# Gate and up products with token rows as output, in the FFNs of a three-block fp32 transformer kernel

## The reference

```
def rmsnorm(x, g):
    xf = x.astype(jnp.float32)
    y = xf * lax.rsqrt(jnp.mean(xf * xf, axis=-1, keepdims=True) + EPS)
    return (y * g.astype(jnp.float32)).astype(x.dtype)

def swiglu(h, w_gate, w_up, w_down):
    return (jax.nn.silu(h @ w_gate) * (h @ w_up)) @ w_down

x = x + 0.5 * swiglu(rmsnorm(x, ffn1_norm[i]), ffn1_w_gate[i], ffn1_w_up[i], ffn1_w_down[i])
```

## Time and profile before

| what | value |
|---|---|
| median of 3 runs | 2114.19 us (2111.84 to 2114.88) |
| span of the profiled execution | 2110.5 us |
| own time of the profiled execution | not reported beside its span |
| PE busy | 1841.2 us, 87% of the span |
| PE weight loads busy | 1364.1 us, 65% |
| DVE busy | 802.8 us, 38% |
| ACT busy | 598.7 us, 28% |
| POOL busy | 133.3 us, 6% |
| granted TensorE clock, mean of the span | 0.924 |
| DMA | 603.95 MB, mean 286 GB/s |

### The profile page before, as it was taken

The page is one execution under the profiler, slowest core; times in us unless marked ns, Lnnn a source line. Parts: engine busy times, 40 slices in busy tenths (PEclk is TensorE's granted clock), DMA queues, the critical chain, the costliest instruction groups (busy, mean ns, idle before and its releaser), DMA issues.

```text
span 2110.5 us, 30801 instructions
## 1 busy us (share of the span) xinstructions
PE 1841.2 (87%) x13330; PEld 1364.1 (65%) x13330; DVE 802.8 (38%) x940; ACT 598.7 (28%) x705; POOL 133.3 (6%) x140
## 2 busy tenths in 40 slices
PE   8999999999999999999999986676777677777766
PEld 8999997999999997699999831222223212122221
DVE  6556556655756564766568500000000000000000
ACT  5334546443433355643347300000000000000001
POOL 4100011400000000220002000000000000000000
PEclk9999999999999999999999987898787879788788
DMA  7555552455555554065566999999999999999998
GB/s 260 189 181 170 162 185 98 168 179 179 201 165 194 195 168 145 21 209 180 179 205 210 423 409 427 429 427 428 429 429 428 428 429 429 428 428 428 429 428 347
DMA packets 182536, 603.95 MB, mean 286 GB/s; under 512 B 11952, under 2 KB 139440, under 8 KB 158016
## 3 DMA queue, kind: packets, MB, share of 16 engines
q1 hardware_dynamic: 180560, 601.43, 73.5%
q10 hardware_dynamic: 1648, 0.96, 0.2%
q0 software_dynamic: 256, 0.52, 0.1%
HBM read 601.84 MB, written 1.05 MB: 286 GB/s over the span
## 4 chain that ended last, share of the span: by engine, by line
PE 59%; DMA 36%; DVE 2%; ACT 1%; issue 1%; SPq 0%; ACTq 0%; POOL 0%; DVEq 0%; POOLq 0%
PE ps L1045 21%; DMA bulk<-in_w_up 17%; PE ps L1059 12%; DMA bulk<-in_w_down 8%; DMA bulk<-in_w_gate 8%; PE ps L1222 3%; PE ps L1618 3%; DMA keep<-in_w_up 2%; PE ps L1644 2%; DMA keep<-in_w_down 2%; PE ps L1116 2%; PE ps L1011 2%; PE ps L1115 2%; PE ps L1117 2%; PE ps L1239 1%; PE ps L1577 1%
## 5 line engine op out<-in xcount | busy, mean ns | idle before, releaser
L1045 PE MATMUL ps<-part,part 128*128 128x256 f32 x3840 | 460.2, 280 | 0.4 <-DVE part L2212 0.4
L1045 PEld LDWEIGHTS ps<-part,part 128*128 128x128 f32 x3840 | 455.5, 188 | 1.0 <-DVE part L2212 0.8
L1618 PE MATMUL ps<-bulk 128*32 128x512 f32 x1616 | 255.8, 765 | 150.6 <-DMA bulk<-in_w_up 93.0
L2212 DVE TENSOR_TENSOR part<-bulk,part 128x2048 fp32r<-128x2048 f32 x88 | 202.9, 2347 | 255.5 <-ACT part L1710 255.5
L1618 PEld LDWEIGHTS ps<-bulk 128*32 128x32 f32 x1616 | 50.8, 125 | 339.4 <-issue 135.1
L1059 PE MATMUL ps<-part,part 128*128 128x256 f32 x2112 | 255.5, 280 | 0.0
L1059 PEld LDWEIGHTS ps<-part,part 128*128 128x128 f32 x2112 | 251.8, 188 | 0.2 <-issue 0.2
L1710 ACT ACTIVATE part<-bulk 128x2048 fp32r<-128x2048 f32 x86 | 160.1, 1910 | 258.0 <-DMA bulk<-in_ffn_w_up 243.8
L2785 DVE TENSOR_TENSOR keep<-keep,ps 128x512 f32<-128x512 f32 x16 | 11.0, 687 | 544.0 <-PE ps L1618 544.0
L1644 PE MATMUL ps<-bulk,keep 128*32 128x512 f32 x784 | 109.4, 693 | 23.6 <-DMA bulk<-in_w_down 23.0
L2221 DVE TENSOR_TENSOR part<-bulk,part 128x2048 fp32r<-128x2048 f32 x46 | 105.6, 2311 | 46.0 <-ACT part L1725 46.0
(11 more groups left out here) (309 smaller groups left out, 2229.8 us busy)
## 6 DMA issues: line engine op xcount, KB each, us to landing
bulk<-in_w_gate SPq DMA_DIRECT2D x53, 2048.0 KB, 40.7
bulk<-in_w_up SPq DMA_DIRECT2D x48, 2048.0 KB, 39.7
bulk<-in_w_down SPq DMA_DIRECT2D x48, 2048.0 KB, 40.2
bulk<-in_ffn_w_gate SPq DMA_DIRECT2D x44, 1024.0 KB, 7.5
bulk<-in_ffn_w_up SPq DMA_DIRECT2D x44, 1024.0 KB, 10.0
bulk<-in_ffn_w_down SPq DMA_DIRECT2D x44, 1024.0 KB, 5.2
keep<-in_w_up SPq DMA_DIRECT2D x16, 2048.0 KB, 40.7
keep<-in_w_down SPq DMA_DIRECT2D x15, 2048.0 KB, 40.4
```

The source lines that it names most:

```text
L1045: ins = pe.matmul(y, w_, x_, start=(k == m == 0), stop=(k == KD - 1 and m == 2))
L1618: ins = pe.matmul(ps[j * CAP:(j + 1) * CAP, half, :], xe[:, k, :], w[:, kk, j * HALF:(j + 1) * HALF], start=(k == 0), stop=(k == KD - 1))
L2212: dve.tensor_tensor(hi(slot(3 * b + i)), slot(3 * b + i), as32(w_hi(f, b, i)), ALU.subtract).then_inc(gu_split, 1)
```

## The change

Gate and up products take the high or low part of x as stationary operand (128 features by 128 tokens) and, as moving operand, 256 gate and 256 up columns side by side (`side_by_side`, an access pattern over two buffers): 512 columns, one whole PSUM bank per token tile `t`, 48 products per chunk instead of 96 of half the width. FFN 0's first chunk keeps products of 256 columns, in the new orientation. The results are token rows, so the norm's factor is one number per partition (`rtok`), applied by ACT in the silu and by DVE in the product of silu and up. The activated rows (`hid_rows`) are then turned to hidden columns by four transposes on TensorE (`turn`), placed in the middle of `down` of the chunk before (for chunk 0 inside gate_up(1)), and ACT and DVE take the high and low part from PSUM. In FFN 0 the turning of the memory tokens (`mem_turn`) moves from the middle to the end of gate_up(1). The loads, and the places of the weight splits in the order of ACT and DVE, are unchanged. The sections that are left out rename buffers (`bulk` becomes `ring` and `arena`; high parts of the weights become contiguous tensors) without moving them.

```diff
+        hid_rows = ffnbuf[:, 0:4 * CW].rearrange("p (b t c) -> p b t c", b=2, t=TT)
...
+        rtok = small[:, 0:TT]
...
+        def side_by_side(a, b):
+
+            return bass.AP(a.tensor, a.offset, [list(a.ap[0]), [b.offset - a.offset, 2]] + [list(d) for d in a.ap[1:]])
...
+            def row_means(n):
+
+                pe.wait_ge(sum_done, n + 1)
+                for t in range(TT):
+                    ins = pe.matmul(bank(4)[:, t:t + 1], sq[:, t * P:(t + 1) * P], mean[:, 0:1], start=(t == 0), stop=True,
+                                    skip_group_check=True)
+                ins.then_inc(rsum_done, 1)
...
-                def terms(b, i, j, k):
-                    w_l, w_h = [w[:, k, j * P:(j + 1) * P] for w in (w_l, w_h)]
-                    return (w_h, hi(xnT)[:, k, :]), (w_h, hi(xT_lo)[:, k, :]), (w_l, hi(xnT)[:, k, :])
+                def weight_parts(b):
+
+                    high, low = [side_by_side(s[0], s[1]) for s in ([w_hi(f, b, i) for i in range(2)],
+                                                                    [hi(slot(3 * b + i)) for i in range(2)])]
+                    return [w.rearrange("p i (k n) -> p i k n", k=KD) for w in (high, low)]
+
+                def rows(b, t):
+                    return ps[:, 2 * b + t, :]
+
+                def terms(b, t, k):
+                    high, low = [w[:, :, k, :] for w in weight_parts(b)]
+                    x_h, x_l = [hi(x_)[:, k, t * P:(t + 1) * P] for x_ in (xnT, xT_lo)]
+                    return (x_h, high), (x_l, high), (x_h, low)
...
+                        for t in range(TT):
+                            for m, (x_, w_) in enumerate(terms(b, t, k)):
+                                ins = pe.matmul(rows(b, t), x_, w_, start=(k == m == 0), stop=(k == KD - 1 and m == 2),
+                                                skip_group_check=True)
+                            if k == KD - 1:
+                                ins.then_inc((gu_half, gu_used)[t], 1)
...
-                    ins.then_inc(gu_used, 1)
+                                if k == KD - 1 and i == 1 and m == 2:
+                                    ins.then_inc((gu_half, gu_used)[t], 1)
                     if f:
-                        mean_square(n, bank(4)).then_inc(rsum_done, 1)
-
-                def gate_up(c, b, between=None):
-                    if not (isinstance(c, int) and c < 2):
-                        pe.wait_ge(gu_free, NCH * f + c - 1)
+                        row_means(n)
+
+                def gate_up(c, b, between={}):
+                    pe.wait_ge(gu_split, (c + NCH * f) * 2 + 2)
+                    for t in range(TT):
+                        for k in range(KD):
+                            if (t, k) in between:
+                                between[t, k]()
+                            for m, (x_, w_) in enumerate(terms(b, t, k)):
+                                ins = pe.matmul(rows(b, t), x_, w_, start=(k == m == 0), stop=(k == KD - 1 and m == 2))
+                        ins.then_inc((gu_half, gu_used)[t], 1)
+
+                def turn(c, b):
+
+                    pe.wait_ge(hid_full, TT * (c + NCH * f + 1))
                     for j in range(2):
+                        for t in range(TT):
+                            ins = pe.transpose(rows(b, 0)[:, j * T + t * P:j * T + (t + 1) * P],
+                                               hid_rows[:, b, t, j * P:(j + 1) * P], ident)
+                    ins.then_inc(hid_turned, 1)
+
+                def down(c, b, first=False, last=False, between=None):
                     pe.wait_ge(dn_split, c + NCH * f + 1)
                     pe.wait_ge(hid_ready, c + NCH * f + 1)
                     for d in range(KD):
+                        if d == KD // 2 and between is not None:
+                            turn(*between)
                         for j in range(2):
...
                     ins.then_inc(dn_used, 1)
 
                 gate_up_first(p)
-                def first_mean():
+                def first_means():
                     pe.wait_ge(const_loaded, 16)
-                    mean_square(0, bank(4)).then_inc(rsum_done, 1)
-
-                gate_up(1, q, between=None if f else (first_mean, mem_turn))
+                    row_means(0)
+
+                gate_up(1, q, {(1, 5): lambda: turn(0, p)} if f else {(0, 4): first_means, (1, 6): lambda: turn(0, p)})
                 if f == 0:
+                    mem_turn()
                     for b in range(4):
                         pe.wait_ge(*out_of(f"mh{b}"))
-                down(0, p, first=True)
+                down(0, p, first=True, between=(1, q))
                 with pe.Fori(1, N_ODD) as i:
                     gate_up(2 * i, p)
-                    down(2 * i - 1, q)
+                    down(2 * i - 1, q, between=(2 * i, p))
                     gate_up(2 * i + 1, q)
-                    down(2 * i, p)
+                    down(2 * i, p, between=(2 * i + 1, q))
                 gate_up(NCH - 1, p)
-                down(NCH - 2, q)
+                down(NCH - 2, q, between=(NCH - 1, p))
                 down(NCH - 1, p, last=True)
...
-                root(bank(4)[:, 0:T])
+                act.activation(rtok, bank(4)[:, 0:TT], ACT.Sqrt, bias=epsc).then_inc(r_root, 1)
...
+                act.wait_ge(r_done, f + 1)
+
                 def chunk(c, b, gu=True, dn=True):
-                    act.wait_ge(ga_done, c + NCH * f + 1)
-                    act.activation(gate_sb[:, b], gate_sb[:, b], ACT.Silu).then_inc(gate_done, 1)
+                    for t in range(TT):
+                        act.wait_ge((gu_half, gu_used)[t], c + NCH * f + 1)
+                        act.activation(hid_rows[:, b, t, :], ps[:, 2 * b + t, 0:CW], ACT.Silu,
+                                       scale=rtok[:, t:t + 1]).then_inc(gate_done, 1)
+                    act.wait_ge(hid_turned, c + NCH * f + 1)
+                    act.activation(hi(hid)[:, b].rearrange("p j t -> p (j t)"), ps[:, 2 * b, :], ACT.Copy).then_inc(hid_hi, 1)
...
-                inverse(n).then_inc(r_done, 1)
+                dve.wait_ge(r_root, n + 1)
+                dve.reciprocal(rtok, rtok).then_inc(r_done, 1)
                 if f == 0:
                     mem_rows_normed()
                 dve.wait_ge(r_done, f + 1)
 
                 def chunk(c, b, gu=True, dn=True):
-                    r2 = rrow.unsqueeze(1).broadcast_to([P, 2, T])
-                    dve.wait_ge(gu_used, c + NCH * f + 1)
-                    dve.tensor_tensor(gate_sb[:, b], ps[:, 2 * b:2 * b + 2, 0:T], r2, ALU.mult).then_inc(ga_done, 1)
-                    dve.tensor_tensor(up_sb, ps[:, 2 * b:2 * b + 2, T:2 * T], r2, ALU.mult).then_inc(gu_free, 1)
-                    dve.wait_ge(gu_free, c + NCH * f + 1)
-                    dve.wait_ge(gate_done, c + NCH * f + 1)
-                    dve.tensor_tensor(gate_sb[:, b], gate_sb[:, b], up_sb, ALU.mult).then_inc(hid_full, 1)
-                    after(dve, dn_used, f, c)
-                    dve.wait_ge(hid_full, c + NCH * f + 1)
-                    dve.tensor_copy(hi(hid)[:, b], gate_sb[:, b]).then_inc(hid_hi, 1)
+                    for t in range(TT):
+                        dve.wait_ge(gate_done, TT * (c + NCH * f) + t + 1)
+                        g = hid_rows[:, b, t, :]
+                        dve.scalar_tensor_tensor(out=g, in0=ps[:, 2 * b + t, CW:2 * CW], scalar=rtok[:, t:t + 1], in1=g,
+                                                 op0=ALU.mult, op1=ALU.mult).then_inc(hid_full, 1)
                     dve.wait_ge(hid_hi, c + NCH * f + 1)
-                    dve.tensor_tensor(hi(hid_lo)[:, b], gate_sb[:, b], as32(hid)[:, b], ALU.subtract).then_inc(hid_ready, 1)
+                    dve.tensor_tensor(hi(hid_lo)[:, b].rearrange("p j t -> p (j t)"), ps[:, 2 * b, :],
+                                      as32(hid)[:, b].rearrange("p j t -> p (j t)"), ALU.subtract).then_inc(hid_ready, 1)
```

More of the change, by code:

```diff
@@ L152, in program @@
         ARENA = 18328
-        bulk, bulk_at = place("bulk", 10 * SLOT + ARENA)
+        ring, ring_at = place("ring", 10 * SLOT)
+        arena, arena_at = place("arena", ARENA)
         keep, keep_at = place("keep", 52736 - 10 * SLOT - ARENA)
-        wring = bulk[:, 0:10 * SLOT]
-        arena = bulk[:, 10 * SLOT:]
-        wall = bulk[:, 0:12 * SLOT]
+        begins = {ring.name: ring_at, arena.name: arena_at, keep.name: keep_at}
         top = [0]
@@ L186, in program @@
         xs = sq.rearrange("p (k t) -> p k t", k=KD)
-        up_sb = sq[:, 2 * T:4 * T].rearrange("p (j t) -> p j t", j=2)
+        rtok = small[:, 0:TT]
         rcol = small[:, 28:30]
         rounded = {}
+        ring_rounded = nc.alloc_sbuf_tensor_at("ring_rounded", [P, 10 * SLOT], F32R, offset=ring_at)
         def hi(ap):
+            if ap.tensor.name == ring.name:
+                return bass.AP(ring_rounded, ap.offset, [list(d) for d in ap.ap])
             n = 1
@@ L197, in hi @@
                 n *= d
[L198 removed]
```

(26 more changed lines are left out.)

21 lines of the change are left out of this document (10 added, 11 removed).

## The result

The changed kernel takes 2460.52 us (median, 2458.49 to 2461.52) against 2113.24 of the kernel before: 1.1645 times, 95% interval 1.163 to 1.1659. The forecast was 2440 in a range of 2370 to 2500.

The account below looks back on a forecast made before the run. TensorE was taken to bound the first half, where the FFNs lie. Full-clock terms of 256 us plus 72 for the clock, 328, on the 2110.5 span gave 2438, or 2442 as median; predicted 2440, range 2370 to 2500.

Parts of the forecast that it names:

- The ring: FFN chunks: turn wait, down's release, loads, splits and next rows form a cycle, 24.1 us against 16.97; 32 cost 230.
- the small chain: FFN 3: the lambda chain on VectorE between the splits and the rows of chunk 2 adds 4.7 us, taken as 5.
- The 5 for turns outside the ring: Turns of chunks 0, 1 and 10 in each FFN: 12 x 0.44 = 5 us added.
- the 6 for width: gate_up of chunks 0, 1 and 10, with wide products: 11 x 0.54 = 6 us gained, bounds 0 and 11.
- the turn of chunk 1 comes after a start with other spacing: Start of each FFN: chunk 1's turn 7.6 or 3.5 us late, mean 5.5; four FFNs make 22.
- the price of 2.0 per wait: Turn and half down after each stall run partly at half clock: 2.0 us lost, 36 stalls, 72, bounds 0 and 119.
- if they come per instruction a wide one takes 224.4: Gate and up: the 11 ns beyond column time is paid once per 512-column product, 224.4 ns, 0.54 us less per chunk.
- A: Rival, chance 0.15: the ring closes, but the clock does not fall, or falls for little; 2370 us.
- B: Rival, chance 0.12: the ring closes and all of turn and half down run at 1.2 GHz; 2489, long landing 2518.
- C: Rival, chance 0.10: gate and up weights land sooner, 9.5 us instead of 11.4, so the ring is shorter; 2381 us.
- D: Rival, chance 0.03: TensorE does not wait at the turn; 2110 us, or 2093 with wide products at 215 ns.

Follow-up runs that it names:

- late turn: Changed kernel with the turn of chunks 1 to 9 moved from the middle of down(c-1) into gate_up(c+1): 2152.01 us.
- load order: Changed kernel with SyncE issuing gate and up loads of chunk c+2 ahead of the down load of chunk c+1: 2164.31 us.
- end turn: Changed kernel with the turn of chunk c directly behind down(c-1), after its release, instead of in its middle: 2258.68 us.
- split order: Changed kernel with the split of down's weights behind the next chunk's silus and products on ScalarE and VectorE: 2370.91 us.
- fill: Changed kernel with 48 unread 128x256 products added mid-down, ahead of the wait for the rows, wherever down has a turn: 2412.62 us.
- The experiment on this start: Changed kernel, but FFN 0's gate_up(1) takes the gate half first in 256-column products, waiting for one split half at a time: 2454.84 us, one execution.

## Why the prediction was right, and what was off

The ring was right in each of its steps. Its links are shown singly: the wait at the turn (late turn: -308 us), the loads behind the end of down (load order: -296), the release that hangs on the turn (end turn: -202), ScalarE's and VectorE's order (split order: -90), the clock (fill: 26.2 to 24.35 on average). The length predicted was 24.1 at full clock and 26.1 with the clock; measured are 24.3 for the filled ring shown above, which has full clock in all its terms, and 26.2.

Split by place, on the spans: the 32 rings and the small chain were put at 230 + 64 + 5 = 299 and took 299.1 us more than the same stretches before. (Eight rings took 208.8, 211.8, 208.8 and 213.2 us in the four FFNs, of which FFN 3 has the small chain; before, the stretch took eight times 16.97, and 0.3 and 0.2 more in FFN 0 and 3.) That this agrees to 0.1 is luck: the ring at full clock is a little longer than predicted, and the clock costs a little less. From the start of an FFN to chunk 1's turn I had put 22 and it was 30.3: 12.8 in FFN 0, 6.9, 5.4 and 5.2 in the others. From the turn of chunk 9 to that of 10 it was 10.8 instead of 8. The last 5.7 us, the seams between an FFN and what follows and 1.1 in the second half, were not in the sum: in FFN 1, where the next gate and up splits stand behind chunk 10's copies, the next FFN's first product starts 1.5 us late. The 5 for turns outside the ring and the 6 for width, which nearly cancel, lie within these pieces.

The step that was mis-sized is "the turn of chunk 1 comes after a start with other spacing": I took the mean of the 7.6 of FFN 1 and the 3.5 of FFN 2, 5.5, for all four, and it measured 7.6 on average. FFN 0 had two things of its own that the diff showed. gate_up(1) waits for both halves of split weights, where before the gate half was enough, so TensorE idled and its clock fell; and ScalarE and VectorE now wait for chunk 0's turn and the memory turn before they split chunk 2 (44.12 instead of 35.63). The experiment on this start moved both (first products at 24.57, split of chunk 2 at 38.99) and gives back 5.1 of the 12.8, the clock's 2.3 among them. How much of the rest is the splits' new place is not shown. I had counted what the change queues behind the new wait on TensorE in the steady loop, and not at the start.

The clock: the price of 2.0 per wait, between 1.7 and 3.3 from the earlier trace rows, was measured at 1.8 to 1.9. The Trainium skill, "TensorE: Matmul & The Clock Gate", section "The HAM clock gate", says that activity lifts the throttle. The filled kernel agrees: its granted clock is 0.99 against 0.85, and it is faster with more work.

Width: "if they come per instruction a wide one takes 224.4" was wrong: a wide product takes 230.4 ns (11.06 us for 48), which is half of the gain expected, so a chunk gains 0.25 us and not 0.54. For the 11 stages on the path that makes 3 us and not 6. By the Trainium skill's N / 2.4 + 2.5 (same page, "Back-to-back issue gap", which calls it the gap of an isolated product) it would be 216, and the trace disagrees. Turns cost 0.44 per four as predicted, 0.87 for eight. So the form as such loses 0.2 us a chunk even where nothing waits.

Rivals: A (no loss by the clock) is excluded by the fill and by the 0.58 of the stretch behind a wait. B (all of turn and half down at 1.2 GHz, 3.3 us per wait) came near in single rings, as where the two take 6.2 us (105.83 to 112.03), but not on average. C needed 9.5 us from the end of down to ScalarE's start and is excluded by the chain, where it is 11.2 (112.03 to 123.27), and D by 36 waits. (With D's 215 ns the gain is 43 x 0.99 = 43 us and its last figure 2091, not 2093.)

## What to carry to other kernels

Before a step is put into an engine's stream, read from the trace how late the other engines are there today. Lateness that a long product stage hides costs nothing until something is asked for sooner. Then follow what hangs on the release behind the new wait, and if the path returns to the wait, price the whole ring rather than the first wait. Do the same at the start of the stage, where the order of the engines is another. Such a ring is opened at its cheapest link: here moving the same four transposes by some 12 us, or issuing two loads ahead of a third instead of behind it, gave back some 300 us. A re-tiling that makes products wider must pay for the transposes it needs: here 0.25 us gained and 0.44 spent per chunk.

## What was not expected of the hardware

An fp32r product of 512 columns takes 230.4 ns at a clock of 1.00, 17 above 512 columns at 2.4 GHz, one of 256 columns 117.8, 11 above: the extra is neither fixed nor proportional. An f32 product of 512 columns takes 429 ns, only 2 above twice its columns at 2.4 GHz. Four turns behind an idle stretch take 0.66 us at a granted clock of 1.00 (filled kernel, 224.01) against 0.44 in unbroken work.
